# Second layer's experts: 96 tokens by gathered rows on VectorE, 160 tokens dense in full-precision products

## The chip, the cores and the metric

One core of a Trainium2 chip runs the kernel. The metric is the device time of one execution in microseconds (us). Each core has TensorE (PE in the profile, its weight loads PEld), VectorE (DVE), ScalarE (ACT), GpSimd (POOL) and SyncE (SP), which here only issues DMAs. The engines run their own instruction streams in order and meet at semaphores.

## The reference

Two blocks of two layers each work on 256 tokens of 1024 channels (`D`). The second block's layers end in a mixture of 128 x 128 experts. The part that matters:

```
def peer(h, w_q, sub_keys, u, v):
    q = (h @ w_q).reshape(T, PEER_HEADS, 2, PEER_QDIM // 2)        # 8 heads, 2 halves, 128 wide
    s = jnp.einsum('thpd,hpnd->thpn', q, sub_keys)
    sv, si = lax.top_k(s, PEER_TOPK)                                # best 16 of 128 keys
    cand = sv[:, :, 0, :, None] + sv[:, :, 1, None, :]              # 16 x 16 pairs
    fv, fi = lax.top_k(cand, PEER_TOPK)                             # best 16 of 256
    ...  idx = i1 * 128 + i2 ;  g = softmax(fv)
    act = gelu(einsum('td,ted->te', hc, u[ic]))                     # 128 experts of 16384 per token
    out = einsum('te,ted->td', gc * act, v[ic])
```

`u` and `v` have 16384 rows of 1024 floats in each layer (64 MB each). Each token picks 8 x 16 = 128 rows of both. Layer 0 runs it on 512 tokens (x and context), layer 1, the last thing in the program, on the 256 of x, followed by a last norm and the output.

## The kernel before

There are two ways to compute the experts, and both are in the program.

Dense: 128 steps, each with one 128 x 1024 tile of `u` (512 KB), give the activations of 128 experts for all tokens ("rise", into two alternating PSUM banks). The picks of each token, as one-hot rows (`mark` on VectorE), are multiplied on TensorE into a 128 x 128 matrix of gates for each token (`gates`, four tokens a step), and activation times gate is multiplied with 128 tiles of `v` ("fall").

Gathered: for 128 tokens at a time, one on each partition, GpSimd issues an indirect DMA (L2601) that brings the p-th chosen row of each token, and VectorE multiplies it with the token and sums (L2617, for `u`) or scales and adds it to a running sum (L2631, for `v`). Such a pair of DMA and VectorE work is a "token step". Five row buffers are in turn; a gather waits until its buffer was used.

Layer 0 (`both_experts`, L2503 to L3012) takes the 256 tokens of x dense and the 256 of the context gathered. Its dense products are full precision (`whole`, L320 to L326): 32-bit operands as they are, each program matmul appearing as two MATMUL records in the profile. Its activations go to DRAM (`act_store`) and come back for `weigh` (L2766), since the gates take the space.

Layer 1 (`experts`, L2004 to L2501) takes all 256 tokens dense with operands split into high and low parts of type fp32r. For each tile ScalarE makes the high part (`split_hi`, L294) and VectorE the low part (`split_lo`, L300). A rise is 8 x 3 products of 256 columns (`three`, L311, L312, L315), a fall 8 products of 512 columns and 8 of 256 (`two`, L336, L339). GpSimd adds the candidate pairs (L2203). The selection on VectorE (`sixteen`: MAX8, FIND_INDEX8, MATCH_REPLACE8; `choose`) runs under the queries and the first 60 rises, the 64 gate steps (L2283 to L2291 marks, L2139 products, L2452 moves to the gate matrix `G`) under rises 62 to 125. Gelu outputs (L2434) go to `act_store` and return for the falls, where VectorE multiplies by the gate (L2313), rounds and rests (L2317, L2319).

All weight tiles come through a ring of four slots (`fetch`: SP waits until the tile four before is done, then issues the next). `mod_norms` (L1745) makes the normed input for layer 1, in two parts, and fetches the first tiles.

Of the kernel before, what the change touches and what calls it, by code (L numbers as in the profile page):

```python
# [25 lines left out]
P = 128  # L26
D = 1024
# [1717 lines left out]
def mod_norms(k, layer, which, streams, ahead, keys=None):  # L1745
# [4 lines left out]
    dst = [k.parts[0]] if S == 1 else [k.stream(m) for m in range(S)]  # L1750
# [8 lines left out]
    with nc.Block() as block:  # L1759
# [8 lines left out]
        def _(act):  # L1768
# [16 lines left out]
            k.split_hi(act, 0)  # L1785
# [14 lines left out]
        def _(dve):  # L1800
# [13 lines left out]
            for n in range(S * KD):  # L1814
                m, c = n // KD, n % KD
                if c == H and m + 1 < S:
                    invert(m + 1)
                if c == 0:
                    dve.wait_ge(rstd.sem, rstd.after(m + 1))
                nc.vector.scalar_tensor_tensor(t[:, n], src[m][:, c], gain[m][:, c:c + 1], stat[:, m, 2],  # L1820
                                               ALU.mult, ALU.mult).then_inc(scaled.sem, 1)
                if n > 1:
                    rest(n - 2)
            rest(S * KD - 2)
            rest(S * KD - 1)
# [178 lines left out]
def experts(k, a, layer, q, keys, m, pending=None, other=None, following=(), next_keys=None, begun=0, finish=None):  # L2004

    nc, HP, NT, B, R = k.nc, 2 * HEADS, T // P, 4, RING
    N, NS, STEPS = NKEYS, UNDER_SELECT, T // 4
    Q, LAG = HP, 4
    wq, u, v, h, parts = a.peer_q[layer], a.peer_u[layer], a.peer_v[layer], k.parts[0], (k.weighted[:], k.hid[:, 0])
    streams, gates_of = (k.x, k.ctx), [k.mods[:, layer, 5 * KD:6 * KD, n] for n in range(2)]
    EARLY, TAIL = EARLY_ADDS, R + (CHUNK_STEP * KD if other is not None else 0)
    LATE = KD - EARLY if pending is not None else 0
    taken, tables = k.count("product_taken"), k.dma("tables_loaded")
    G = k.region(0, NKEYS, T)  # L2020
    s, left = k.region(6144, NT * HP, NKEYS), k.region(10240, NT * HP, NKEYS)
    cand, cand_left = k.region(14336, NT * HEADS, 256), k.region(18432, NT * HEADS, 256)
    pick = [k.region(22528, NT * P, 16), k.region(14336, NT * P, 16)]
    o = 26624
    sv, si, sif = k.region(o, NT * HP, 16), k.region(o + 512, NT * HP, 16).bitcast(U32), k.region(o + 1024, NT * HP, 16)
    fv, fi = k.region(o + 1536, NT * HEADS, 16), k.region(o + 1792, NT * HEADS, 16).bitcast(U32)
    part = k.region(o + 2048, 2, NT * P).bitcast(U32)
    partf = k.region(o + 2560, 2, NT * P)
    chosen = k.region(o + 3072, 2, NT * P)
    weight = k.region(o + 3584, NT * HEADS, 16)  # L2030
    wsum = k.region(o + 3840, 2, NT * HEADS)
    FINAL = (11, 17, 20)
    done, acted, scored, moved, top, pairs, after, exps, transposed, picked = map(k.count, (
        "tile_done", "gelu_done", "key_scores", "key_scores_moved", "top_step", "pair_scores", "pick_step", "weight_exp",
        "picks_turned", "picks_kept"))
    marked, marks_weighted, product, kept, parted = map(k.count, (
        "keys_marked", "marks_weighted", "gate_product", "gate_kept", "weight_parted"))
    inverted = k.count("other_inverted")
    weighted, rounded, ready, summed, added = map(k.count, ("expert_weighted", "hidden_hi", "hidden_ready", "sums_complete",
                                                            "half_added"))  # L2040
    both_halves = sv.rearrange("p (n two) b -> p n two b", two=2)
    sides = sif.rearrange("p (n two) b -> p n two b", two=2)
    by_block = s.rearrange("p (t r) n -> p t r n", t=NT)
    marks = k.scratch[:].bitcast(BF16).rearrange("p (r m a n t) -> p r m a n t", r=2, m=4, a=2, t=2)
    keys_in_twos = k.c("twos").bitcast(BF16).rearrange("p (n t) -> p n t", t=2).unsqueeze(1).to_broadcast([P, 4, NKEYS, 2])
    pairs_of_picks = k.picks[:].rearrange("p s m (a t) -> p s m a t", t=2)
    rests = k.scratch[:, 0:2 * T].rearrange("p (r s t) -> p r s t", r=2, t=B)
    act_in = k.scratch[:, 0:R * T].rearrange("p (r t) -> p r t", r=R)
    hid = k.scratch[:, R * T:(R + 2) * T].rearrange("p (r t) -> p r t", r=2)
    falls = [(k.ps[:, c], c) for c in (0, 1, 2, 3, 6, 7, 4, 5)]  # L2050
    turns = (N - TAIL) // R
    chunk = k.acts[:, 2:4]
    settled, totalled, rstd, normed, stored = k.count("x_settled"), k.count("squares_summed"), k.count("rstd"), k.count("normed"), k.dma("stored")
    exp_under = 0

    with nc.Block() as block:
        @block.sync
        def _(sp):
            def act_load(r, i, free, e):

                sp.wait_ge(weighted.sem, i * R + weighted.after(free))
                sp.dma_start(act_in[:, r], k.act_store[e]).then_inc(k.act_loaded[r].sem, 16)

            for j in range(R, Q + R):
                k.fetch(sp, j, 0, wq[j] if j < Q else u[j - Q])
            for e in range(N):
                j = e + R
                k.fetch(sp, Q + j, 0, u[j] if j < N else v[:, j - N])
                sp.wait_ge(acted.sem, acted.after(e + 1))
                sp.dma_start(k.act_store[e], k.acts[:, e % R]).then_inc(k.act_stored[e % R].sem, 16)  # L2070
                if e == NS + STEPS + GATES_LAG:
                    sp.wait_ge(product.sem, product.after(STEPS))
                    for r in range(R):
                        sp.wait_ge(k.act_stored[r].sem, k.act_stored[r].after(16))
                        act_load(r, 0, 0, r)
            for r in range(R):
                sp.wait_ge(k.act_stored[r].sem, k.act_stored[r].after(16 * (N // R)))
            with sp.Fori(0, turns) as i:
                for r in range(R):
                    k.fetch(sp, Q + N + R + r, i, v[:, i * R + (R + r)])  # L2080
                    act_load(r, i, r + 1, i * R + (R + r))
            for r in range(TAIL - R):
                k.fetch(sp, Q + N + R + r, turns, v[:, (turns + 1) * R + r])
                act_load(r % R, turns, r + 1, (turns + 1) * R + r)
            if next_keys is not None:
                sp.wait_ge(weighted.sem, turns * R + weighted.after(1))
                sp.dma_start(keys, next_keys).then_inc(tables.sem, 16)
            for r, tile in enumerate(following):
                if r < R - 1:
                    k.fetch(sp, Q + N + TAIL + r, turns, tile)  # L2090
                else:
                    sp.wait_ge(summed.sem, summed.after(KD))
                    sp.dma_start(k.ring[:, k.slot(r)], tile).then_inc(k.loaded[k.slot(r)].sem, 16)
            if finish is not None:
                for n in range(KD // 2):
                    c = slice(2 * n, 2 * n + 2)
                    sp.wait_ge(normed.sem, normed.after(2 * n + 2))
                    sp.dma_start(k.out[:, c], k.x[:, c]).then_inc(stored.sem, 16)
                sp.wait_ge(stored.sem, stored.after(16 * (KD // 2)))

        @block.tensor
        def _(pe):
            def query(j):

                pe.wait_ge(taken.sem, taken.after(j + 1 - R))
                if pending is not None and EARLY <= j < R:
                    pe.wait_ge(settled.sem, settled.after(LATE_ADDS.index(j) + 1))
                k.three(pe, j, 0, [(k.ps[:, j % R, 0:T], c, h[:, 0, c], h[:, 1, c]) for c in range(KD)],
                        True).then_inc(done.sem, 1)

            def score(p):

                pe.wait_ge(taken.sem, taken.after(2 * p + 2))
                pe.wait_ge(moved.sem, moved.after(p - 1))
                if p == 0:
                    pe.wait_ge(tables.sem, tables.after(16))
                if pending is not None and p < 2:
                    pe.wait_ge(settled.sem, settled.after(LATE_ADDS.index(6 + p) + 1))
# [29 lines left out]
            for j in range(Q + NS):  # L2148
                if j < Q:
                    query(j)  # L2150
                else:
                    rise(j - Q)
# [1118 lines left out]
```

## Time and profile before

| | us |
|---|---|
| runs | 3851.36, 3845.62, 3851.86 (median 3851.36) |
| the profiled execution | 3843.3, span 3841.5 |
| PE busy | 3526.2 (92%) |
| DVE busy | 2646.4 (69%) |
| ACT busy | 1190.2 |
| POOL busy | 636.1 |
| second layer's experts: first product to the end | 2990.0 to 3841.5 |

The profile's times count from the span's start. Layer 0's experts lie at about 1560 to 2800, layer 1's at 2990 to the end. A busy time is the union of an engine's instructions; the duration of one instruction includes its way through the pipeline, so that in a merged timeline row "x8" the distance from start to start is (row's time - one duration) / 7. PEclk is the granted clock, 1.00 being 2.4 GHz.

### The profile page before, as it was taken

How to read it: one execution, taken by the hardware profiler on the slowest of the kernel's cores; microseconds unless marked ns; L12 is line 12 of the kernel's file. 1: busy time of each engine (PE TensorE's matmuls, PEld its weight loads, DVE VectorE, ACT ScalarE, POOL GpSimd, SP SyncE). 2: the span in 40 equal slices, each digit the busy share in tenths (PEclk: the TensorE clock that was granted, in tenths of full speed). 3: DMA queues.
4: the chain of work that ended last, by engine and by line, in shares of the span. 5: the costliest groups of instructions: out<-in, count | busy, mean ns of one | idle time of the engine just before them, and what ended most of it. 6: DMA issues, size and time to landing. Idle time of an engine off the chain costs nothing. (4 is left out here: it accounts for less than half of the span.)

```text
span 3841.5 us, 61464 instructions
## 1 busy us (share of the span) xinstructions
PE 3526.2 (92%) x23498; PEld 3088.3 (80%) x23498; DVE 2646.4 (69%) x4823; ACT 1190.2 (31%) x1934; POOL 636.1 (17%) x564
## 2 busy tenths in 40 slices
PE   9998999989999879998499988788888999999999
PEld 9976999977988658886488766666676999998887
DVE  5665656646663464699888667677755698887887
ACT  4345334334442342110122100000035444543333
POOL 0000000001000010044555455555500000000000
PEclk9999999999999999999799999999999999999999
DMA  7652666634652113389899999999921576557776
GB/s 245 225 194 88 236 210 216 227 117 143 229 167 92 43 60 123 105 337 388 285 367 365 343 396 401 400 404 402 402 77 50 178 227 206 181 184 225 233 233 193
DMA packets 298398, 882.90 MB, mean 230 GB/s; under 512 B 32928, under 2 KB 99488, under 8 KB 297248
## 3 DMA queue, kind: packets, MB, share of 16 engines
q1 hardware_dynamic: 224416, 610.93, 47.0%
q0 software_dynamic: 73728, 268.47, 18.0%
q8 instruction: 173, 2.83, 0.3%
q14 instruction: 81, 0.66, 0.1%
HBM read 842.57 MB, written 36.70 MB: 229 GB/s over the span
## 5 line engine op out<-in xcount | busy, mean ns | idle before, releaser
L300 DVE TENSOR_TENSOR ring_lo<-ring,ring_hi 128x1024 fp32r<-128x1024 f32 x637 | 781.2, 1227 | 449.6 <-ACT ring_hi L294 429.7
L294 ACT ACTIVATE ring_hi<-ring 128x1024 fp32r<-128x1024 f32 x637 | 675.3, 1060 | 1032.4 <-PE banks L315 753.6
L325 PE MATMUL banks<-scratch,ring 128*128 128x256 f32 x2048 | 501.1, 403 | 118.7 <-DVE scratch L2766 118.5
L311 PE MATMUL banks<-h_parts,ring_hi 128*128 128x256 f32 x2312 | 575.9, 287 | 5.8 <-PEq L664 2.9
L325 PEld LDWEIGHTS banks<-scratch,ring 128*128 128x128 f32 x2048 | 403.7, 201 | 216.2 <-DVE scratch L2766 158.5
L312 PE MATMUL banks<-h_parts,ring_hi 128*128 128x256 f32 x2312 | 566.1, 283 | 0.0
L325 PE MATMUL banks<-h_whole,ring 128*128 128x256 f32 x2048 | 466.2, 385 | 60.9 <-ACT acts_out L2956 55.9
L325 PEld LDWEIGHTS banks<-h_whole,ring 128*128 128x128 f32 x2048 | 386.7, 192 | 117.5 <-ACT acts_out L2956 57.6
L311 PEld LDWEIGHTS banks<-h_parts,ring_hi 128*128 128x128 f32 x2312 | 442.0, 191 | 18.7 <-issue 17.8
L312 PEld LDWEIGHTS banks<-h_parts,ring_hi 128*128 128x128 f32 x2312 | 442.5, 191 | 0.3
L315 PE MATMUL banks<-h_parts,ring_lo 128*128 128x256 f32 x2312 | 325.2, 283 | 1.5 <-DVE ring_lo L300 1.4
L315 PEld LDWEIGHTS banks<-h_parts,ring_lo 128*128 128x128 f32 x2312 | 298.0, 192 | 3.4 <-DVE ring_lo L300 3.4
L311 PE MATMUL banks<-h_parts_ctx,ring_hi 128*128 128x256 f32 x768 | 189.9, 285 | 4.3 <-ACT ring_hi L294 4.3
L312 PE MATMUL banks<-h_parts_ctx,ring_hi 128*128 128x256 f32 x768 | 187.7, 282 | 0.0
L2601 POOL DMA_INDIRECT x_t<-peer_rows_dram,rows x103 | 128.1, 1244 | 349.2 <-DVE rows L2715 211.6
L2631 DVE SCALAR_TENSOR_TENSOR h_whole<-x_t,rows,h_whole 128x1024 f32<-128x1024 f32 x102 | 130.8, 1283 | 61.4 <-DMA x_t<-peer_v_dram,rows 60.8
L2631 DVE SCALAR_TENSOR_TENSOR h_whole<-ctx_t,rows,h_whole 128x1024 f32<-128x1024 f32 x101 | 129.6, 1286 | 55.8 <-DMA ctx_t<-peer_v_dram,rows 54.5
L2956 ACT ACTIVATE acts_out<-banks 128x256 f32<-128x256 f32 x128 | 48.9, 384 | 383.7 <-PE banks L325 379.9
L1775 ACT ACTIVATE big<-x_t 128x1024 f32<-128x1024 f32 x4 | 4.0, 1048 | 521.3 <-PEq L2561 515.9
L312 PE MATMUL banks<-hidden_parts,ring_hi 128*128 128x256 f32 x672 | 162.9, 281 | 0.0
L311 PE MATMUL banks<-hidden_parts,ring_hi 128*128 128x256 f32 x672 | 162.8, 281 | 0.0
L984 POOL TENSOR_TENSOR scratch<-ctx_t 128x256 f32<-128x256 f32 x8 | 7.9, 990 | 927.6 <-POOLq L609 927.6
(352 smaller groups left out, 6146.3 us busy)
## 6 DMA issues: line engine op xcount, KB each, us to landing
ring<-peer_u_dram SPq DMA_DIRECT2D x256, 512.0 KB
ring<-peer_v_dram SPq DMA_DIRECT2D x256, 512.0 KB
big<-mod_w_dram SPq DMA_DIRECT2D x96, 512.0 KB, 4.5
ring<-ffn_gate_dram SPq DMA_DIRECT2D x88, 512.0 KB
ring<-ffn_up_dram SPq DMA_DIRECT2D x88, 512.0 KB
ring<-ffn_down_dram SPq DMA_DIRECT2D x88, 512.0 KB
act_store<-acts_out SPq DMA_DIRECT2D x256, 128.0 KB
scratch<-act_store SPq DMA_DIRECT2D x256, 128.0 KB
```

The costliest lines, as they stand in the source:

```text
L294: self.nc.scalar.activation(self.hi[:, n % 2], self.ring[:, self.slot(j)], ACT.Copy).then_inc(self.count("tile_hi").sem, 1)
L300: self.nc.vector.tensor_tensor(self.lo[:, self.slot(j)], self.ring[:, self.slot(j)], self.hi[:, n % 2].bitcast(F32), ALU.subtract).then_in ...
L311: self.nc.tensor.matmul(out, w, b_hi, start=opens and m == 0, stop=False)
L312: self.nc.tensor.matmul(out, w, b_lo, start=False, stop=False)
L315: ins = self.nc.tensor.matmul(out, self.lo[:, self.slot(j), c * P:(c + 1) * P], b_hi, start=False, stop=opens and m == last)
L325: ins = self.nc.tensor.matmul(out, self.ring[:, self.slot(j), c * P:(c + 1) * P], b, start=opens and m == 0, stop=opens and m == len(terms ...
L984: k.nc.gpsimd.tensor_tensor(to, norm.src[:, c], norm.src[:, c], ALU.mult).then_inc(squared.sem, 1)
L1775: nc.scalar.activation(sq[:, m * KD + n * H:m * KD + (n + 1) * H], src[m][:, n * H:(n + 1) * H], ACT.Square).then_inc(squares.sem, 1)
L2601: nc.gpsimd.indirect_dma_start(bufs[n % ROWS], None, rows_of[n // TOKEN_STEPS], bass.IndirectOffsetOnAxis(idx[:, t, p:p + 1], 0)).then_inc ...
L2631: nc.vector.scalar_tensor_tensor(tok[:, t], bufs[b], coef[:, t, p:p + 1], tok[:, t], ALU.mult, ALU.add).then_inc(used.sem, 1)
L2956: nc.scalar.activation(k.acts[:, e % R], k.ps[:, 4 + e % 2, 0:T], ACT.Gelu).then_inc(acted.sem, 1)
```

## The change

`experts` goes, `split_experts` takes its place for layer 1 with S = 96: tokens 0 to 95 are gathered, tokens 96 to 255 (DENSE = 160 columns) are dense. `mod_norms(..., whole=True)` writes one full-precision input. Every product takes `whole`, so no tile is split. The 160 columns of all 128 activations fit in `A` (20480 words a partition), so they stay in SBUF: no `act_store`. The gates come for half of the 128 first-key columns at a time: 40 steps of four tokens (64 columns a product) under the rises from the 66th on, which gate `A[:, 0:64]` in place, and 40 more under the first 56 falls, which gate `A[:, 64:128]`. The first `A` columns that lie on the scores `s` (`AT_SCORES` = 51) have to wait for the last selection level. The candidate adds move from GpSimd to VectorE; GpSimd issues 256 gathers. The tables for gathering cover both layers. Layer 0's code is the same but for those table names.

```
-def experts(k, a, layer, q, keys, m, pending=None, other=None, following=(), next_keys=None, begun=0, finish=None):
...
+def split_experts(k, a, layer, S, finish):
+    DENSE, G = T - S, HEADS // 2
+    N, Q, STEPS, HALF = NKEYS, 2 * HEADS, DENSE // 4, NKEYS // 2
+    A = k.region(0, NKEYS, DENSE)
+    s, AT_SCORES = k.region(8192, NT * HP, NKEYS), 8192 // DENSE
+    order = [(table, p) for table in range(2) for p in range(P)]
+    EXP_AT, SELECTED, FIRST_GATES = 62, 64, 66
+    gates_after = [[n for n in range(STEPS) if FIRST_GATES + n * (N - 1 - FIRST_GATES) // STEPS == e] for e in range(N)]
+    gates_under = [[n for n in range(STEPS, 2 * STEPS) if (n - STEPS) * (HALF - 8) // STEPS == r] for r in range(N)]
...  sync
+            for j in range(R, Q):
+                k.fetch(sp, j, 0, wq[j])
+            for e in range(N):
+                k.fetch(sp, U + e, 0, u[e])
+            for e in range(N):
+                k.fetch(sp, V + e, 0, v[:, e])
...  gpsimd: 256 gathers of 96 rows
+                pool.wait_ge(used.sem, used.after(n + 1 - ROWS))
+                nc.gpsimd.indirect_dma_start(bufs[n % ROWS], None, rows_of[table],
+                                             bass.IndirectOffsetOnAxis(idx[:, p:p + 1], 0)).then_inc(...)
...  vector: a v row now adds to one sum and waits for the step before it
+                    dve.wait_ge(used.sem, used.after(n))
+                    nc.vector.scalar_tensor_tensor(tok, bufs[b], coef[:, p:p + 1], tok, ALU.mult, ALU.add).then_inc(used.sem, 1)
+            def spend(columns):
+                if units:
+                    spent += columns + 150
+                    if spent >= 1200 and step < min(P, 32 * units):
+                        spent -= 1200
+                        token_step()
+            def mark(n):      # second: 512 columns; in_half: 256, 512 and 256 columns
+            def weigh(n):
+                acts = A[:, h * HALF:(h + 1) * HALF, n_of_half * B:(n_of_half + 1) * B]
+                dve.wait_ge(product.sem, product.after(n + 1))
+                nc.vector.tensor_tensor(acts, acts, k.ps[:, gate_bank(n), 0:B * HALF]..., ALU.mult).then_inc(kept.sem, 1)
+            for t in range(NT):
+                for b in range(G):      # 8 units: 4 rows of 128 keys, then the choices of 2 heads
+                    level(t, b)
+                    LEVELS = count
+                    SETTLED = choices(t, b)
...
+            for n in range(2 * STEPS + 1):
+                if n < 2 * STEPS:
+                    mark(n)
+                if n:
+                    weigh(n - 1)
+                for _ in range(1 + (n % 3 < 2) if n < STEPS else 1 + n % 2):
+                    if step < (P if n < STEPS else len(order)):
+                        token_step()
+            while step < len(order):
+                token_step()
...  tensor
+            def rise(e):
+                pe.wait_ge(acted.sem, acted.after(e - 1))
+                k.whole(pe, U + e, [(k.ps[:, 4 + e % 2, 0:DENSE], c, hx[:, c, S:T]) for c in range(KD)], True).then_inc(done.sem, 1)
+            for r in range(N - 1):
+                if r == HALF:
+                    pe.wait_ge(kept.sem, kept.after(2 * STEPS))
+                fall(r).then_inc(done.sem, 1)
+                for n in gates_under[r]:
+                    gates(n)
+            pe.wait_ge(used.sem, used.after(len(order)))
+            for c in range(KD):
+                nc.tensor.transpose(back[:, c, 0:S], tok[:, c * P:(c + 1) * P], ...).then_inc(turned_back.sem, 1)
+            pe.wait_ge(settled.sem, settled.after(KD))
...  scalar
+            for e in range(N):
+                if e == AT_SCORES:
+                    act.wait_ge(top.sem, top.after(LEVELS))
+                if e == EXP_AT:
+                    act.wait_ge(after.sem, after.after(SETTLED))
+                    nc.scalar.activation(weight, weight, ACT.Exp).then_inc(exps.sem, 1)
+                act.wait_ge(done.sem, done.after(U + e + 1))
+                nc.scalar.activation(A[:, e], k.ps[:, 4 + e % 2, 0:DENSE], ACT.Gelu).then_inc(acted.sem, 1)
...
-    mod_norms(k, 1, 1, (0,), first(a.peer_q[1]), a.peer_k[1])
-    peer(k, a, 1, 0, finish=k.v("final"))
+    mod_norms(k, 1, 1, (0,), first(a.peer_q[1]), a.peer_k[1], True)
+    split_experts(k, a, 1, 96, k.v("final"))
```

## Rows read from the trace of the kernel before

**Rows 1.** The page, part 1: busy time and share of each engine.
```profile
PE 3526.2 (92%) x23498; PEld 3088.3 (80%) x23498; DVE 2646.4 (69%) x4823; ACT 1190.2 (31%) x1934; POOL 636.1 (17%) x564
```
**Rows 2.** Windows: stretch; length; busy time by engine; clock; DMA share; GB/s.
```profile
core 0: us, PE busy (x) PEld busy (x) DVE busy (x) ACT busy (x) POOL busy (x), PEclk, DMA share, GB/s
2990.00:3048.00 58.00, 57.97 (x487) 58.00 (x488) 37.09 (x113) 27.63 (x42) 3.33 (x4) 1.00 0.49 154
3048.00:3464.00 416.00, 414.49 (x3805) 409.39 (x3804) 347.44 (x633) 203.71 (x325) 7.21 (x12) 1.00 0.63 200
3464.00:3826.00 362.00, 360.69 (x2054) 314.55 (x2053) 293.88 (x513) 135.19 (x128) 0.00 (x0) 1.00 0.75 228
```
**Rows 3.** Groups of instructions, 3000 to 3841: count, busy us, mean ns, idle before.
```profile
L300 DVE TENSOR_TENSOR ring_lo<-ring,ring_hi 128x1024 fp32r<-128x1024 f32 x268 | 328.7, 1227 | 77.2 <-ACT ring_hi L294 74.8
L294 ACT ACTIVATE ring_hi<-ring 128x1024 fp32r<-128x1024 f32 x268 | 284.5, 1061 | 460.0 <-PE banks L315 237.4 <-PE banks L339 222.6
```
**Rows 4.** Chain that ended last, falls: start, us, what; 128 such pairs.
```profile
3473.23 1.86 PE banks L336 x8
3476.04 1.86 PE banks L336 x8
```
**Rows 5.** TensorE timeline: products of 256, 128 (scores) and 128 (gates) columns.
```profile
2167.69 3.62 PE L325 MATMUL banks<-h_whole,ring 128*128 128x256 f32 x16
...
3008.26 1.06 PE L2121 MATMUL banks<-big 128*128 128x128 f32 x8
...
2102.08 0.85 PE L2873 MATMUL banks<-scratch 128*128 128x128 bf16 x12
```
**Rows 6.** VectorE timeline: selection and a gathered row between two operations.
```profile
3014.53 0.87 DVE L2233 MAX8 big<-big 128x8 f32<-128x128 f32 x4
...
1667.31 0.75 DVE L2652 MAX8 big<-big 128x8 f32<-128x256 f32 x2
...
1703.12 2.29 DVE L2709 TENSOR_TENSOR big<-big 128x2048 f32<-128x2048 f32 x1
1705.33 1.22 DVE L2617 CUSTOM_DVE_ANT_0 rows<-rows,h_whole 128x1024 f32<-128x1024 f32 x1
1706.47 0.08 DVE L2617 DVE_READ_ACCUMULATOR2_ANT rows<- 128x1 f32 x1
```
**Rows 7.** VectorE timeline: marks of one gate step in layer 0.
```profile
1956.92 0.69 DVE L2739 TENSOR_TENSOR scratch<-scratch,picks 128x1024 bf16<-128x1024 bf16 x1
1957.65 0.42 DVE L2743 TENSOR_TENSOR scratch<-scratch,picks 128x512 bf16<-128x512 bf16 x1
1957.99 1.22 DVE L2617 CUSTOM_DVE_ANT_0 rows<-rows,h_whole 128x1024 f32<-128x1024 f32 x1
```
**Rows 8.** Layer 0's stall for the selection: timelines of ScalarE and TensorE.
```profile
1862.18 0.42 ACT L2962 ACTIVATE big<-big 128x256 f32<-128x256 f32 x1 [55.75 <-DVE big L2712]
...
1864.35 5.33 PE L325 MATMUL banks<-h_whole,ring 128*128 128x256 f32 x16 [52.73 <-ACT acts_out L2956]
```
**Rows 9.** Windows of L325 alone: PE and PEld busy, clock, DMA share, GB/s.
```profile
1860.00:1910.00 50.00, 33.28 (x129) 27.14 (x130) 0.82 0.91 319
1910.00:1960.00 50.00, 43.90 (x192) 35.33 (x192) 1.00 0.99 365
```
**Rows 10.** Windows of layer 0's falls: all engines, then L2631 alone.
```profile
2310.00:2360.00 50.00, 41.30 (x169) 33.68 (x168) 36.27 (x37) 0.00 (x0) 29.29 (x25) 0.93 1.03 400
...
2310.00:2360.00 50.00, 33.16 (x27) 0.93 1.03 400
```
**Rows 11.** DMA queues, 2400 to 2600: packets, MB, share of the 16 engines.
```profile
q0 software_dynamic: 14238, 51.85, 65.7%
q1 hardware_dynamic: 11870, 28.38, 36.8%
```
**Rows 12.** The page, part 5: gathered rows added to a sum.
```profile
L2631 DVE SCALAR_TENSOR_TENSOR h_whole<-ctx_t,rows,h_whole 128x1024 f32<-128x1024 f32 x101 | 129.6, 1286 | 55.8 <-DMA ctx_t<-peer_v_dram,rows 54.5
L2601 POOL DMA_INDIRECT x_t<-peer_rows_dram,rows x103 | 128.1, 1244 | 349.2 <-DVE rows L2715 211.6
```
**Rows 13.** VectorE timeline at the end: last additions, reciprocal, final scaling.
```profile
3828.04 0.47 DVE L946 SCALAR_TENSOR_TENSOR x_t<-banks,mods,x_t 128x256 f32<-128x256 f32 x1
...
3833.38 1.75 DVE L434 RECIPROCAL big<-big 128x256 f32<-128x256 f32 x1
3835.62 3.25 DVE L2409 SCALAR_TENSOR_TENSOR x_t<-x_t,vec,big 128x256 f32<-128x256 f32 x8 [0.48 <-ACT big L441]
```

More of the change, by code:

```diff
@@ L1742, in summed_norm, with mod_norms @@
     rstd_ends(k)
-def mod_norms(k, layer, which, streams, ahead, keys=None):
+def mod_norms(k, layer, which, streams, ahead, keys=None, whole=False):
     nc, H, S = k.nc, KD // 2, len(streams)
-    dst = [k.parts[0]] if S == 1 else [k.stream(m) for m in range(S)]
+    dst = [k.whole_parts] if whole else [k.parts[0]] if S == 1 else [k.stream(m) for m in range(S)]
     squares, summed, mean, inverse, rstd, scaled, rounded = map(k.count, (
@@ L1784, in _ @@
                         root(m + 1)
-            k.split_hi(act, 0)
+            if not whole:
+                k.split_hi(act, 0)
         @block.tensor
@@ L1821, in _ @@
                                                ALU.mult, ALU.mult).then_inc(scaled.sem, 1)
-                if n > 1:
+                if n > 1 and not whole:
                     rest(n - 2)
-            rest(S * KD - 2)
-            rest(S * KD - 1)
+            if not whole:
+                rest(S * KD - 2)
+                rest(S * KD - 1)
     squares.ends(2 * S)
@@ L2507, in both_experts @@
     wq, u, v = a.peer_q[layer], a.peer_u[layer], a.peer_v[layer]
-    rows_of = (a.peer_rows, v.rearrange("a b d -> (a b) d"))
+    rows_of = (a.peer_rows, a.peer_v.rearrange("l a b d -> (l a b) d"))
     gates_of = [k.mods[:, layer, 5 * KD:6 * KD, m] for m in range(2)]
@@ L3104, in even_mixer @@
                   a.peer_k[0])
-def peer(k, a, layer, m, **more):
-    experts(k, a, layer, k.region(0, 2 * HEADS, T), keys_of(k), m, **more)
 def peer_0(k, a):
@@ L3251, in layouts @@
     out["peer_v"] = i["peer_v_2"].reshape(2, NKEYS, NKEYS, D)
-    out["peer_rows"] = i["peer_u_2"][0]
+    out["peer_rows"] = i["peer_u_2"].reshape(2 * NKEYS * NKEYS, D)
     return {n: np.ascontiguousarray(v) for n, v in out.items()}
```

772 lines of the change are left out of this document (328 added, 444 removed).

## Prediction

> **What bounds the kernel now.** I read the page's busy times first: TensorE is busy for 92% of the span [rows 1]. Then I cut the last stage into stretches. The reader is to see that TensorE has no gap in it: 57.97 of 58 us in the queries, 414.5 of 416 in the rises, 360.7 of 362 in the falls, at full clock, while the DMAs move 154 to 228 GB/s [rows 2]. VectorE is busy for 83% of rises and falls, most of it low parts of tiles (268 of 1.23 us), and ScalarE makes as many high parts of 1.06 us; both keep up [rows 3]. The chain of waits says the same for the falls: the next group of products starts 2.81 us after the last, 128 times, which makes 360 us [rows 4]. A rise is as long (24 products of 256 columns where a fall has 8 x 512 + 8 x 256 = 24 x 256). So the stage is as long as its products, and the change is worth what it does to them, less what it makes late.
>
> **Cost of a full-precision product.** Layer 0 shows the form to come. Sixteen records of 256 columns take 3.62 us with the last one's 0.38, so start to start is (3.62 - 0.38) / 15 = 0.216 us; of 128 columns (scores) eight take 1.06, one 0.275: 0.112 us [rows 5]. A line through both gives 0.138 at 160 columns. Two records a product, 8 products: 16 x 0.138 = 2.2 us a tile in place of 2.81. Bounds: 0.112 (the shorter row) and 0.216 (nothing shrinks). I take the line, since both rows lie close to one price a column (0.84 and 0.875 ns).
>
> **Removed.** All splitting (268 x 1.23 us of VectorE, 1.06 of ScalarE) and all traffic of activations through DRAM; neither was on the path. On the path: 256 x (2.81 - 2.2) = 156 us. Of `mod_norms`, the second parts and the first split_hi (1.06 us) and half its VectorE steps: I put the start 3 us earlier, at 2987 (between 0 and 6).
>
> **Added on TensorE.** Queries are full width: 16 x 16 x 0.216 = 55.3 us against 16 x 2.81 = 45, so +10. Gate steps: 80 of 12 products of 64 columns instead of 64 of 128 columns. Twelve of 128 columns take 0.85 us with 0.22 for the last, so 0.057 each [rows 5]. No row has 64 columns. Ends: 0.028 (half) and 0.057 (the weight load of 128 columns, which stays, sets it). I take 0.057: 80 x 0.69 = 55 us and 0.05 a step for changing over, 59. Transposes of tokens and picks: 3 us.
>
> **VectorE, selection.** It now decides when TensorE may go past rise 52: the activations from the 51st on lie on the scores, ScalarE waits for the last level, and rise 53 waits for ScalarE. A row of 128 keys: MAX8 start to start (0.87 - 0.28) / 3 = 0.20; two of them, two indices, one replacement and three value loads of 0.06 make 1.16 us, four rows 4.7. A row of 256 candidates at 0.33 makes 1.85, two 3.7. An operation of 2048 elements takes 2.21 to the next start, so 512 take about 0.6; seven (six picks, one candidate add) 4.2 [rows 6]. Small ones and waits for own results about 1.7. A unit: 14.3 us; there are eight. Between them `spend` places gathered rows: a unit counts 16,578 columns, over 1200 that is 13.8 rows, in seven units 97. One costs 1.14 us [rows 6], 15.9 a unit. Unit 1 starts at 3012, when the scores of two heads are there (6 queries of 3.46, transposes, scores: 25 us) and ends at 3026; the other seven end at 3026 + 7 x 30.2 = 3237, the last level 19 before, 3218. I add 6 for rows that arrive late: 3224.
>
> TensorE is at the end of rise 52 at 2987 + 55 + 10 + 53 x 2.2 = 3169, so it stands for 55 us. Layer 0 has the same sight: ScalarE waited 55.75 us for the selection and TensorE 52.73 behind it [rows 8]. After it, the clock was 0.82 over 50 us and 129 records of L325 were made where the next window has 192 [rows 9]; with the 4 us until it resumed and without gate steps, some 10 us of work were lost. So +10, which takes the restart to 3234.
>
> **From there TensorE should run through.** 75 rises 165 us, 40 gate steps 30, transposes and waits 3: 3432. VectorE must do a gate step in 4.0 us here: marks of 512, 256, 512 and 256 columns, where a 512 one takes 0.34 to 0.38 [rows 7]: 1.2; weighing 256 columns 0.45; rows 1.67 x 1.14 while the 26 left of `u` last: 3.6 us. Falls: 128 x 2.2 = 282, 40 gate steps 30, openings 2. A step comes every 3.8 us; VectorE needs 1.65 + 1.5 x 1.32 (each `v` row now waits for the sum before it, 1.286 [rows 12] and 0.03) = 3.6. It fits, so both lots of marks are hidden; if that cover went, each 0.1 us of a step would cost 4 us in a half.
>
> **DMA at the end.** Rows move 96 x 4 KB = 0.393 MB, tiles 0.524. From the restart on, tiles every 2.2 us and rows of a gate step make 350 to 360 GB/s. Layer 0's falls run at 400 GB/s with the DMA engines full [rows 10], and both queues pay the same there: 65.7% for 51.85 MB, 36.8% for 28.38, 1.3% a MB [rows 11]. So these stretches fit. But after the 80th step (about 3583) VectorE has 68 rows left and takes them back to back: 298 GB/s beside 239 of the tiles. With 73 falls to go (160 us) and 62.9 MB to move (156 us), an equal split of 400 gives a row every 1.96 us (layer 0: 27 of 0.524 MB in 50 us [rows 10]) and a tile every 2.61. 68 rows last 133 us, 51 tiles pass; 22 more take 48: 181 us, +21.
> The Trainium skill (DMA: Bandwidth & Descriptors, Queues, rings and completion order) says that each DMA engine takes its queue rows in turn, a packet at a time; that would give the equal split. No run here shows both queues backlogged. The same page (Specifications) gives 358 GB/s as a core's share of HBM, which speaks against this change; by that figure, an estimate, the last stretch would be 198 us and not 181. The trace, with 400 over whole windows, does not agree.
>
> **Tail.** Eight additions of 160 columns (3 us), eight of 96 (2.2), squares and their sum only after all of these (0.5 + 3.5 to 7), mean, reciprocal 1.75, root, scaling 3.25 [rows 13], output 2.5: 19 us, 15.5 before.
>
> **Sum.** 3234 + 198 + 314 + 21 + 19 = 3786 against a span of 3841.5: -55. The profiled execution took 3843.3, so 3788; the median of the runs is 8 above it, so I predict 3796.
>
> **Rivals.**
> A. Cheaper still. Gate products of 64 columns at 0.028 take 26 us off, the tiles keep their full rate at the end (-21), the clock recovers sooner (-5). For it: loads overlap products everywhere. With most of them: 3755.
> B. Rows first. The gather queue takes what it asks for: 68 rows in 90 us, tiles get 100 GB/s meanwhile (17), the other 56 at 2.2: 213 us instead of 181, +32; in the selection the rows come late, too, 97 by up to 0.3, so the stall is longer by up to 20. 3828 to 3848. For it: GpSimd can issue a gather in about 1.24 us [rows 12], so up to five are outstanding; against: in layer 0 the rows were what waited (54.5 us on one buffer pair).
> C. Slower: a product of 160 columns doesn't shrink. If a floor from the 32-bit weight loads (0.19 us each in the profile) held, the 4096 records cost 0.19 instead of 0.138: +213, time 4009. It decides from 0.151 us a record, where the gain is gone. Against: 128 columns run at 0.112 with such loads.
> D. Slower: VectorE sets the pace of both halves. From 0.7 us over TensorE's 3.8 and 4.0 a step the 80 steps eat the 55 us; that needs 4.5 to 4.7 us. If each dependent mark and the in-place weighing (runs of four elements) showed its full duration, 1.65 would become 2.1, and with rows as late as in layer 0's falls (1.92) a step of the second half takes 2.1 + 1.5 x 1.92 = 5.0 (+1.2 x 40 = 48) and one of the 16 steps that still have `u` rows 2.1 + 1.67 x 1.92 = 5.3 (+21): 3865. Against: layer 0's gate steps, with 1.79 us of marks and 1.67 rows, were not late for TensorE [rows 7, 9].
>
> **Chances.** The forecast's case 0.55 (its own range 3770 to 3822), A 0.13, B 0.15, C 0.04, D 0.10, others slower 0.03. A measurement here can tell 0.2% from no change, which is 8 us: faster by more than that 0.81 (forecast, A, most of B), within it 0.06 (rest of B, part of D), slower 0.13. Range for 8 in 10: from A's middle to where B ends and D begins, 3750 to 3850.
>
> **What would show each step.** L325 records of 160 columns in the second layer 0.138 apart; gate records of 64 columns 0.057 or less; one idle of TensorE behind ScalarE's wait for VectorE near 3169, some 55 us, then a window of low clock; no long wait of `gates` for the marks; after the 80th step DMA share 1.0 at 400 GB/s and TensorE waiting on tiles of `v`; rows done before the last fall. The prediction is wrong if the records are above 0.15, if the idle at rise 53 is above 90 us, or if gate steps wait on VectorE in most falls.

## The result, and the profile after

The kernel after takes 3947.27 us (median of 4 runs, 3941.21 to 3954.46), the kernel before 3848.49 (4 runs, 3841.83 to 3851.86): a ratio of 1.026, 95% interval 1.0235 to 1.0284. I had said 3796 and faster. The profiled execution took 3954.46 us, its span is 3952.7. The page of after, parts 1 and 4 (the first against [rows 1]; before, part 4 gave PE 21%, DVE 1% and DMA 0%):

```profile
PE 3386.4 (86%) x22534; PEld 2962.0 (75%) x22551; DVE 2524.7 (64%) x4839; ACT 878.7 (22%) x1601; POOL 877.8 (22%) x804
...
DMA 15%; PE 7%; DVE 2%; issue 0%; ACT 0%; SPq 0%; DVEq 0%; POOLq 0%
```

TensorE has 140 us less to do, as intended, and the chain of waits now runs through DMAs. Windows of after (columns as in [rows 2]: busy time of PE, PEld, DVE, ACT, POOL, clock, DMA share, GB/s):

```profile
3100.00:3150.00 50.00, 32.18 (x216) 29.42 (x215) 38.07 (x103) 3.95 (x13) 16.25 (x17) 1.00 1.03 274
3250.00:3300.00 50.00, 18.98 (x111) 18.59 (x109) 44.63 (x133) 1.71 (x6) 19.18 (x21) 0.66 0.84 225
3450.00:3500.00 50.00, 50.00 (x490) 49.47 (x489) 22.04 (x66) 6.12 (x21) 0.00 (x0) 1.00 0.73 216
3800.00:3850.00 50.00, 33.68 (x222) 30.55 (x223) 22.37 (x18) 0.00 (x0) 15.90 (x18) 1.00 1.03 280
```

Read the last two columns together. In the first and the last window the DMA engines are full (1.03) and move 274 and 280 GB/s. In layer 0 the same share moved 400 [rows 10]. The third window, where `u` rows have ended and `v` rows are not yet allowed (GpSimd x0), is the stage as I had drawn it: TensorE busy for 50.00 of 50 us. The timeline of TensorE in after shows both kinds: while rows come, a tile's 16 records take 2.41 us and then wait for the next tile; without rows they follow each other.

```profile
3205.75 2.41 PE L325 MATMUL banks<-h_whole,ring 128*128 128x160 f32 x16 [1.64 <-DMA ring<-peer_u_dram]
3209.66 2.41 PE L325 MATMUL banks<-h_whole,ring 128*128 128x160 f32 x16 [1.49 <-DMA ring<-peer_u_dram]
...
3482.34 0.52 PE L2836 MATMUL banks<-scratch 128*128 128x64 bf16 x12
3482.70 2.42 PE L325 MATMUL banks<-h_whole,ring 128*128 128x160 f32 x16
3484.95 0.52 PE L2836 MATMUL banks<-scratch 128*128 128x64 bf16 x12
```

A tile passes every 3.9 us (3209.66 - 3205.75) instead of 2.25 (3484.95 - 3482.70). By groups, TensorE waited 100 us for tiles of `u` and 102 for tiles of `v` in after's last stage:

```profile
L325 PE MATMUL banks<-h_whole,ring 128*128 128x160 f32 x2048 | 308.7, 306 | 132.7 <-DMA ring<-peer_u_dram 100.0 <-ACT big L2914 31.6 <-issue 1.0
L325 PE MATMUL banks<-big,ring 128*128 128x160 f32 x2048 | 308.6, 306 | 103.7 <-DMA ring<-peer_v_dram 101.9 <-issue 1.6
```

### The profile page after: what moved, and what is told of

Same layout as the page of the kernel before. It is cut to its first block and busy times, and to the rows that moved or that the text cites. A ratio compares the mean times of both kernels' runs of the same rounds, so it can differ in the third digit from the quotient of the medians.

```text
span 3952.7 us, 56964 instructions
## 1 busy us (share of the span) xinstructions
PE 3386.4 (86%) x22534; PEld 2962.0 (75%) x22551; DVE 2524.7 (64%) x4839; ACT 878.7 (22%) x1601; POOL 877.8 (22%) x804
## 3 DMA queue, kind: packets, MB, share of 16 engines
q0 software_dynamic: 102400, 369.15, 27.2%
## 5 line engine op out<-in xcount | busy, mean ns | idle before, releaser
L325 PE MATMUL banks<-h_whole,ring 128*128 128x256 f32 (+1 forms) x4352 | 830.8, 347 | 196.1 <-DMA ring<-peer_u_dram 103.4
L325 PEld LDWEIGHTS banks<-h_whole,ring 128*128 128x128 f32 x4352 | 720.0, 192 | 274.5 <-ACT big L2914 82.2
L300 DVE TENSOR_TENSOR ring_lo<-ring,ring_hi 128x1024 fp32r<-128x1024 f32 x365 | 448.0, 1228 | 369.0 <-ACT ring_hi L294 352.9
L325 PE MATMUL banks<-scratch,ring 128*128 128x256 f32 x2048 | 494.1, 398 | 127.2 <-DVE scratch L2269 126.9
L325 PEld LDWEIGHTS banks<-scratch,ring 128*128 128x128 f32 x2048 | 397.2, 198 | 224.3 <-DVE scratch L2269 169.6
L294 ACT ACTIVATE ring_hi<-ring 128x1024 fp32r<-128x1024 f32 x365 | 386.7, 1060 | 569.7 <-PE banks L315 515.2
L325 PE MATMUL banks<-big,ring 128*128 128x160 f32 x2048 | 308.6, 306 | 103.7 <-DMA ring<-peer_v_dram 101.9
L325 PEld LDWEIGHTS banks<-big,ring 128*128 128x128 f32 x2048 | 284.3, 192 | 122.3 <-DMA ring<-peer_v_dram 118.9
L311 PE MATMUL banks<-h_parts,ring_hi 128*128 128x256 f32 x1160 | 288.1, 286 | 7.4 <-PEq L664 4.5
L312 PE MATMUL banks<-h_parts,ring_hi 128*128 128x256 f32 x1160 | 284.9, 283 | 0.0
L311 PEld LDWEIGHTS banks<-h_parts,ring_hi 128*128 128x128 f32 x1160 | 222.4, 192 | 19.2 <-issue 18.8
L312 PEld LDWEIGHTS banks<-h_parts,ring_hi 128*128 128x128 f32 x1160 | 222.5, 192 | 0.3
L315 PE MATMUL banks<-h_parts,ring_lo 128*128 128x256 f32 x1160 | 163.5, 284 | 0.1
L311 PEld LDWEIGHTS banks<-h_parts_ctx,ring_hi 128*128 128x128 f32 x768 | 146.6, 191 | 13.8 <-issue 13.5
```

Of the source, the lines that this page charges most:

```text
L294: self.nc.scalar.activation(self.hi[:, n % 2], self.ring[:, self.slot(j)], ACT.Copy).then_inc(self.count("tile_hi").sem, 1)
L300: self.nc.vector.tensor_tensor(self.lo[:, self.slot(j)], self.ring[:, self.slot(j)], self.hi[:, n % 2].bitcast(F32), ALU.subtract).then_in ...
L311: self.nc.tensor.matmul(out, w, b_hi, start=opens and m == 0, stop=False)
L312: self.nc.tensor.matmul(out, w, b_lo, start=False, stop=False)
L315: ins = self.nc.tensor.matmul(out, self.lo[:, self.slot(j), c * P:(c + 1) * P], b_hi, start=False, stop=opens and m == last)
L325: ins = self.nc.tensor.matmul(out, self.ring[:, self.slot(j), c * P:(c + 1) * P], b, start=opens and m == 0, stop=opens and m == len(terms ...
```

## The experiments

Every kernel starts from after; ratios are against the kernel before on the same chip. To compare transfers I use one price: DMA engines that are full and move R GB/s spend 16 x 4096 B / R on 4 KB, which is 0.160 us at 409 GB/s and 0.237 at 277.

**Rows of 128 in place of 96** (`e1_rows128`). The gather fills all 128 partitions; VectorE still uses 96. More bytes, everything else alike. (In the cuts of code "..." stands for what is left out.)

```diff
-    idx, ... = k.rows[0:S, 1, 0:P].bitcast(U32), ...
-    first_row = k.rows[0:S, 1, 3 * P:4 * P]
+    idx, ... = k.rows[:, 1, 0:P].bitcast(U32), ...
+    first_row = k.rows[:, 1, 3 * P:4 * P]
-                nc.gpsimd.indirect_dma_start(bufs[n % ROWS], None, ...
+                nc.gpsimd.indirect_dma_start(full[n % ROWS], None, ...
...  (full: the same buffers with all 128 partitions; the indices are made for 128 tokens)
```

> Each gather brings 128 rows (also those of tokens 96 to 127) into all 128 partitions; VectorE still uses 96. A third more bytes are gathered. Theory (spread): 96 rows don't lie evenly on the 16 DMA engines and the memory's entries, so packets of both queues take 0.24 us instead of 0.16. Then with 128 rows packets go back to 0.16, the DMAs to 400 GB/s, tiles of u come every 2.6 us or faster, and the time falls to 3790 to 3840. Rival (bytes: this stage's tables or this mix give only 280 GB/s): 34 MB more at 280 GB/s, +120: about 4070.

3789.66 us (4 runs, 3786.42 to 3798.08), ratio 0.9853 (0.983 to 0.9875): with a third more bytes in each gather the kernel is 158 us faster than after. That is at the lower edge of what I expected if packets fall back to 0.16 us, and far from the 4070 of the rival that looks at bytes. Windows of this kernel, columns as above:

```profile
3100.00:3150.00 50.00, 46.09 (x306) 42.09 (x307) 43.35 (x134) 5.99 (x20) 19.36 (x20) 1.00 1.03 409
3600.00:3650.00 50.00, 46.96 (x309) 42.16 (x307) 25.36 (x20) 0.00 (x0) 17.82 (x20) 1.00 1.03 409
```

The share is the same 1.03 as in after, the rate 409 GB/s, and L325's waits for tiles fall from 202 us to 13:

```profile
L325 PE MATMUL banks<-h_whole,ring 128*128 128x160 f32 x2048 | 303.6, 304 | 66.0 <-ACT big L2915 53.8 <-DMA ring<-peer_u_dram 6.6
L325 PE MATMUL banks<-big,ring 128*128 128x160 f32 x2048 | 307.7, 304 | 13.5 <-DMA ring<-peer_v_dram 6.7
```

Such waits are understated: a tile before a wait shows 2.41 us, where tiles without one are 2.25 apart, as its last product shows its whole 0.30 us.

**The same queues, side by side.** In after, 3750 to 3850, and in e1, 3100 to 3200 (packets, MB, share of the 16 engines):

```profile
q1 hardware_dynamic: 3904, 14.23, 52.1%
q0 software_dynamic: 3904, 13.72, 50.7%
```
```profile
q0 software_dynamic: 5785, 21.06, 52.9%
q1 hardware_dynamic: 5373, 19.52, 49.0%
```

Both queues are dearer in after, the tiles' (q1, always 128 partitions) as much as the rows' (q0): 52.1% for 14.23 MB is 3.7% a MB, 49.0% for 19.52 is 2.5%. So a narrow gather also slows the transfers beside it. And after's two queues take packet for packet, 3904 and 3904, which is the equal split that the forecast assumed. The Trainium skill (DMA: Bandwidth & Descriptors, Queues, rings and completion order) says that each DMA engine takes its queue rows in turn, a packet at a time; this row agrees.

**64 rows** (`e2c_rows64`) and **112 rows** (`e7_rows112`).

```diff
+                nc.gpsimd.indirect_dma_start(bufs[n % ROWS][0:64 if n >= ROWS else S], None, ...   # e2c, its u steps read the token twice
+                nc.gpsimd.indirect_dma_start(full[n % ROWS][0:112], None, ...                      # e7, indices for 112 tokens
```

> After the first five, each gather brings only 64 of its 96 rows, to partitions 0 to 63 (the u steps read the token twice). Spread theory: packets of both queues stay at 0.24 us or above, and the DMAs move no more, or fewer, GB/s than with 96 rows (230 to 280) although a third of the gathered bytes is gone; the time falls only as the packets get fewer, to 3830 to 3880. Bytes theory: 280 GB/s, 33 MB less, -120: 3830. A fixed limit on gathered packets alone: packets below 0.2 us, DMA not full, 3800.

> Each gather brings 112 rows into partitions 0 to 111, VectorE uses 96. 64 rows gave packets of 0.29 us, 96 of 0.24, 128 of 0.16. Two forms of the spread theory. (a) Share: the slow part of the memory's entries gets more than its share of the rows, and 112 is nearer to even: packets 0.19 to 0.21, 320 to 350 GB/s, time between the two, 3840 to 3890. (b) Fit: only 128 rows, 8 for each DMA engine, go each engine to its own entry, and 7 an engine are as crooked as 6: packets stay at 0.23 or above, under 290 GB/s, and with 17% more gathered bytes the time is above 3947, near 3990.

64 rows: 3915.03 us (2 runs, 3904.59 to 3925.47), ratio 1.0175 (1.0136 to 1.0214), above all three times that I had expected (3830 to 3880, 3830, 3800). 112 rows: 4008.14 (2 runs), 1.0424 (1.0403 to 1.0445), case (b) of what I expected. The queues of 112 rows, 3100 to 3200:

```profile
q1 hardware_dynamic: 3901, 14.21, 51.7%
q0 software_dynamic: 3902, 13.98, 51.0%
```

112 rows pay what 96 do (3.6% a MB in both queues), so the price does not slide evenly from 96 rows to 128: 128 is cheap, and 112 is as dear as 96. With 64 rows, the windows 3100:3150 and 3600:3650 move 233 and 240 GB/s at a share of 1.03, some 0.28 us for 4 KB, dearer still. The rows have a third fewer packets; I take it, without a run that shows it, that this is why that kernel still beats after. That 112 rows cost 61 us more than 96 fits the price of the added packets: as an estimate, 256 gathers x 16 packets at 0.23 us over 16 engines are 59 us, if the DMAs are full wherever rows run.

**Is it the row gather alone, or two queues that meet?** (`e8_rows_alone`: tiles of `u` and `v` bring 16 of 128 partitions, each gather its 96 rows.)

```diff
+                sp.dma_start(k.ring[0:16, k.slot(j)], src).then_inc(k.loaded[k.slot(j)].sem, 16)
...  (the same for u)
-                k.fetch(sp, V + e, 0, v[:, e])
+                part_of(V + e, v[0:16, e])
```

> Tiles of u and v bring only 16 of their 128 partitions (7/8 of each is left out); queries and the gathers of 96 rows are whole. If a gather of 96 rows is slow by itself (its own packets meet at the entries), its 4 KB packets take over 0.2 us with almost nothing beside them; if it is slow only against the tiles' packets, they take 0.16. Either way TensorE waits for no tile and the time is that without gathers, 3720 to 3740.

3731.71 us (2 runs, 3727.85 to 3735.57), ratio 0.9705 (0.9686 to 0.9724). The rows' queue, 3600 to 3650, here and in e1:

```profile
q0 software_dynamic: 2919, 10.25, 87.9%
```
```profile
q0 software_dynamic: 2835, 10.33, 51.9%
```

The same bytes, brought 96 at a time with almost nothing beside them, take 87.9% of the DMA engines' time instead of 51.9%. That is 0.28 us for 4 KB, so the narrow gather is slow without whole tiles beside it. (It was not quite alone: the other queue, with its 16-partition tiles, took 13.5%.) In after, gathers and tiles together fill the engines, and TensorE waits.

**No gathers** (`e3c_nogather`: those after the fifth are left out; VectorE does as many operations, those of `u` on the token alone).

```diff
-            for n, (table, p) in enumerate(order):
+            for n, (table, p) in enumerate(order[:ROWS]):
```

> Only the first five gathers are issued; the other 251 are left out, VectorE does the same operations on what lies in the buffers (the u steps read the token twice). If the gathers' traffic is the whole loss, tiles come every 2.2 us, no wait of TensorE for DMA is left, one stall for the selection at rise 53 of about 50 us remains, and the time is 3745 to 3775. If VectorE's work or the selection order were the loss, it stays above 3850.

3726.55 us (2 runs), ratio 0.9685 (0.9661 to 0.971), 19 us under the range that I had given. In the last stage TensorE has one long wait, 51.4 us for the selection, and none for tiles. Timelines of TensorE in after, e1 and e3c (start, length, idle before and what ended it):

```profile
3286.95 13.14 PE L325 MATMUL banks<-h_whole,ring 128*128 128x160 f32 x80 [31.02 <-ACT big L2914]
```
```profile
3244.33 10.35 PE L325 MATMUL banks<-h_whole,ring 128*128 128x160 f32 x64 [53.41 <-ACT big L2915]
```
```profile
3228.90 29.13 PE L325 MATMUL banks<-h_whole,ring 128*128 128x160 f32 x192 [51.38 <-ACT big L2916]
```

**The whole change with 128 tokens by rows** (`e4_s128`): a gather of 128 rows that is used whole, and products of 128 columns.

```diff
-    split_experts(k, a, 1, 96, k.v("final"))
+    split_experts(k, a, 1, 128, k.v("final"))
```

> The split at 128 tokens: 128 gathered, 128 dense. Spread theory: packets 0.16 us, 400 GB/s; products of 128 columns 0.112 us apart, 64 gate steps, and from the end of the selection (3237) 178 MB at 400 GB/s are what lasts: end near 3705, 3700 to 3760, some 3% faster than the kernel before. Rival (bytes): 280 GB/s: about 3880 to 3900. Rival (VectorE sets the pace): 3542 is where it would be done, so no.

3776.09 us (4 runs, 3774.35 to 3783.06), ratio 0.9813 (0.9795 to 0.983), slower than the 3700 to 3760 that I had expected. The split at 128 brings 14 us over e1. TensorE is busy for only 39.62 of 50 us in 3600:3650 (46.96 in e1), at the same 409 GB/s: the DMAs bound this version too, by their volume.

**Later selection, earlier rows** (`e5_s128_scores_apart`, `e6_v_rows_early`), both with 128 tokens by rows like e4. e5 puts the scores where no activation has to wait for them and moves the points at which TensorE turns to the selection's results from rises 62, 64 and 66 to 74, 76 and 78. e6 also lets rows of `v` start 20 gate steps into the rises, for which ScalarE makes the gathered tokens' gelu at rise 108 and not after the last.

```diff
-    s, AT_SCORES = k.region(8192, NT * HP, NKEYS), 8192 // DENSE
+    s, AT_SCORES = k.region(16384, NT * HP, NKEYS), N
-    EXP_AT, SELECTED, FIRST_GATES = 62, 64, 66
+    EXP_AT, SELECTED, FIRST_GATES = 74, 76, 78
-                    if step < (P if n < STEPS else len(order)):
+                    if step < (P if n < 20 else len(order)):     # e6 only
...  (e6: the gelu of the gathered tokens at e == 108)
```

> The split at 128, with the scores above the 128 activations (so no rise waits for the last selection level) and the picks taken at rise 76 instead of 64. The 51 us stall of e4 goes, and the DMAs, the bound there, are full in that time: 259 MB at 409 GB/s from 3026 on, plus some 25 us of rises without rows, plus the tail: 3700 to 3735. If the stall was hidden by the DMA bound, nothing changes: 3776.

> As e5, and rows of v may come from the 20th gate step on (the gathered tokens' gelu is made at rise 108 instead of after the last), so the stretch of rises without gathers goes: 10 to 25 us less than e5, 3680 to 3715. If the end of the products and not the DMAs sets the time there, no gain over e5.

e5: 3759.99 us (4 runs, 3757.73 to 3766.88), ratio 0.9783 (0.9766 to 0.9799). e6: 3747.28 (4 runs, 3741.94 to 3752.42), ratio 0.975 (0.9734 to 0.9766), the fastest kernel here that does the whole work, some 200 us under after. Both times lie above what I had expected (3700 to 3735 and 3680 to 3715). By the ratios, which take out the change of chip, e5 gains 12 us over e4, and e6 13 over e5. TensorE's idle before the selection shrank from 51.34 us in e4 to 26.09 in e5 and 25.88 in e6. ScalarE's wait behind it, in e4, e5 and e6:

```profile
ACT big L2912 <- DVE big L2703: 53.7, 1, 53.7
```
```profile
ACT big L2912 <- DVE big L2703: 27.5, 1, 27.5
```
```profile
ACT big L2912 <- DVE big L2703: 27.3, 1, 27.3
```

L2912 is the `exp`. Already in e4, where activations reach the scores only at rise 64, it was the `exp` before rise 62 that stood, and not the activations on the scores for which I had blamed it. What e5 took away is therefore the 12 rises by which the `exp` comes later; what moving the scores is worth alone, no run shows. Windows of e6:

```profile
3350.00:3400.00 50.00, 45.22 (x484) 43.91 (x483) 37.61 (x76) 5.74 (x21) 17.75 (x15) 0.97 0.95 348
3600.00:3650.00 50.00, 39.88 (x312) 36.08 (x311) 25.40 (x20) 0.00 (x0) 18.45 (x19) 1.00 1.03 409
```

In e5 the first of these stretches moved 265 GB/s at a share of 0.83. e6 fills it, and in the second the DMAs are full as before: there TensorE (busy for 39.88 of 50 us) waits for tiles.

## Why the prediction was wrong

The failed step is in the part **DMA at the end**: "Layer 0's falls run at 400 GB/s with the DMA engines full [rows 10], and both queues pay the same there: 65.7% for 51.85 MB, 36.8% for 28.38, 1.3% a MB [rows 11]. So these stretches fit." Those are gathers of 128 rows. I carried their price to gathers of 96, scaled only by bytes, and put no bounds around it, although no row of before shows a gather of fewer than 128 partitions. What the runs showed in its place is 0.237 us for 4 KB in both queues, and TensorE waiting 202 us for tiles. The falls show what it cost, as an estimate: 128 tiles and about 128 rows of 96 are 128 x (128 + 96) = 28,672 packets. At 0.160 us over 16 engines that is 287 us, less than the 314 of the products; at 0.237 it is 425 us, and the falls took 425. So close a match is chance, since the first tiles and rows were fetched before the falls and the last 42 us ran without rows; the size is not.

The rest of the sum can be read from e1, the same kernel with the price that I had assumed. Times are in us from each span's start; L325's first and last records and the restart behind ScalarE's wait mark them. The forecast's restart is taken as 3224, without the 10 us that it added there for the clock; they stand in its rises here, where such a loss would be seen.

| mark | forecast | e1 | after |
|---|---|---|---|
| first product of the queries | 2987 | 2992 | 2994 |
| restart after the selection | 3224 | 3244 | 3287 |
| end of rises | 3432 | 3438 | 3510 |
| end of falls | 3767 | 3773 | 3936 |
| end of span | 3786 | 3789 | 3953 |

After is 167 us above the forecast: 7 at the start, 56 from there to the restart (293 against 237), 15 in the rises (223 against 208), 91 in the falls (426 against 335), and the tail 2 shorter. The steps one by one:

- **Start**: said 3 us earlier than before's 2990. It was 2993.89 in after, 2991.63 in e1 and 2998.82 in e3c; the code ahead of it is the same in the three, so this says nothing of a gain.
- **Products**: said 0.138 us a record, measured (2.41 - 0.30) / 15 = 0.141. Right; rival C (0.19) is out.
- **Gate products**: said 0.057, and 0.69 us for twelve. From the first to the next product it is 3482.70 - 3482.34 = 0.36 us, 0.030 each, rival A's end of the range. 80 steps cost 29 us and not 59. e1's total does not show this gain, and its match with the forecast is partly luck: in e1's falls 128 tiles and about 128 rows of 128 are 32,768 packets, 328 us at 0.160 of the 333 measured, so its falls are bound by DMAs that the forecast's smaller gathers would not have needed; without gathers the same falls took 298 (e3c). With 96 rows at 0.160 (287 us) and gate products at 0.030 the falls would have been shorter than my 335; no run here shows that, since no narrow gather ran at that price.
- **Selection and stall**: said a stall of 55 us, and 237 us from the first product to the restart, 6 of them for rows that come late. Without gathers the stall was 51.38 and the stretch 3228.90 - 2998.82 = 230, so the selection itself (231) was right. With gathers of 128 rows they were 53.41 and 3244.33 - 2991.63 = 253: late rows cost 23 us, not 6. In after the stall is 31.02 only because TensorE, slowed by tiles, came to the wait 65 us later than in e1 (3256 against 3191), while the selection, slowed by rows, was 43 us later.
- **Clock after the stall**: said 10 us, measured 2. In e3c the granted clock was 0.50, that is 1.2 GHz, while TensorE stood (3190 to 3228) and in the 4 us after its restart, where 12 records were made; from 3236 on it was 1.00, with 32 records in 4 us. The first 192 records took 29.13 us, where 191 x 0.141 + 0.30 makes 27.2. In after it was 0.66 over 3250 to 3300, 31 us of which TensorE stood. The row behind the 10 us [rows 9] holds something else too: in before, TensorE stood a second time from 1870 to 1879 (8.83 us, L2906 behind VectorE's L2728), and the 10 us include that. The 8 us too many here hide part of the 17 too few for late rows.
- **VectorE's pace**: it did not set it. In after VectorE waited 117.3 us for the gate products (`L2743` behind `PE banks L2836`), the other way round from rival D, and in e1, with tiles on time, gate products waited 5.3 us in all for the marks.
- **Equal split at the end**: right in after, packet for packet, with the packet's price wrong.
- **Tail**: said 19, measured 17.

None of the signs that I named as proof of error appeared: records under 0.15, idle under 90, gate steps on time. I had watched the engines and not the DMA rate outside the last stretch; "400 GB/s at a share of 1.0" was listed only for the time after the 80th step.

Measured, with tiles beside them, were 0.237 / 0.160 = 1.48 at 96, 1.45 at 112 (283 GB/s) and 1.75 at 64 (233 GB/s), and 1.75 for 96 nearly alone (e8). The runs agree on the direction and on none of the sizes, least of all at 112. The same skill (DMA: Bandwidth & Descriptors, Back-pressure in remote DMA) says of transfers between cores that stalled writes stall an engine's other queues too; the equal rise of q1's price is what that would look like here, for local transfers, but no run here shows that this is the reason.

What makes 96 and 112 rows slow inside the chip (ports, or how packets are dealt to the DMA engines) stays open: the traces give the engines' mean and no run held the one fixed while the other changed. Every gather here began at partition 0, so the number of rows and the partitions that they fill were not told apart either, and no run narrowed the tiles while the gathers stayed whole. That the gather's width is the cause is shown by e1 and e7: more rows of the same kind made after 158 us faster at 128 and 61 us slower at 112.

## What to carry to other kernels

Price a DMA by its shape, not by its bytes: where the change makes a gather narrower than any in the trace, its rate is an unknown that needs bounds. A sum of DMA demand belongs beside every stretch that the change makes faster, not only at its end. And a narrow gather is paid for by every transfer beside it; bringing 32 rows that nobody reads made the kernel 158 us faster here than leaving them out.

## What the runs showed that I had not expected

- In windows of 50 us with the DMA engines full (share 1.01 or more), they moved, with whole tiles beside the gathers, 395 to 410 GB/s with gathers of 128 rows, 267 to 293 with 112, 266 to 282 with 96, 226 to 262 with 64.
- Gathers of 96 rows almost alone filled the DMA engines at 236 GB/s (e8, 3600 to 3650, share 1.02).
- TensorE's products of 64 columns with weights of 128 x 128 followed each other every 0.030 us; those of 128 columns every 0.057 [rows 5].
